# Attention outputs computed transposed, two heads on column halves, with the arena and the opening laid out anew

## The reference

```python
x = layer_norm(ALPHA * x + 0.5 * swiglu_ffn(x, ffn1_w_up, ffn1_w_down), ln1_g, ln1_b)
x = layer_norm(ALPHA * x + hybrid_mixer(x, ...), ln2_g, ln2_b)
x = layer_norm(ALPHA * x + 0.5 * swiglu_ffn(x, ffn2_w_up, ffn2_w_down), ln3_g, ln3_b)
```

```python
logits = where(valid, q . k * scale + bias, -1e30)
p = softmax(logits)
y = sum over keys of p * v
```

## Time and profile before

| | |
|---|---|
| time, median of 3 runs | 1142.32 us (1141.85 to 1142.46) |
| the profiled execution | 1143.03 us; span in the trace 1141.1 us |
| granted TensorE clock, mean | 0.998 |
| TensorE busy | 1128.2 us, 99% |
| VectorE, ScalarE, GpSimd busy | 764.8, 556.1, 409.2 us |
| matmuls of `split_mm` with `xh`, `xl` (lines 712 to 714) | 1236.6 us of busy time, overlapping |
| the same with `hh`, `hl` | 419.0 us |

### The profile page before, as it was taken

One profiled execution on the slowest core, in us unless ns is written; L12 is line 12 of the kernel. 1 busy time (PEld: TensorE's weight loads), 2 busy tenths in 40 slices (PEclk: granted clock), 3 DMA queues, 4 the chain that ended last, 5 costly groups with the idle time before them and its releaser, 6 DMA issues.

```text
span 1141.1 us, 17628 instructions
## 1 busy us (share of the span) xinstructions
PE 1128.2 (99%) x5916; PEld 923.9 (81%) x5916; DVE 764.8 (67%) x1078; ACT 556.1 (49%) x799; POOL 409.2 (36%) x567
## 2 busy tenths in 40 slices
PE   8999999999999999999999999999999999999997
PEld 6788887878788888887788888888777888888885
DVE  5666845789976866685486465468898687655544
ACT  5544542575573455453245454335846635454530
POOL 2789976107710378997700000001276000000001
PEclk9999999999999999999999999999999999999999
DMA  8856653645555575666357566536435466757541
GB/s 266 236 183 195 216 193 111 192 144 160 161 181 196 172 232 177 193 217 201 115 176 227 186 223 199 186 98 222 162 118 183 148 202 199 223 166 242 186 145 37
DMA packets 158719, 207.50 MB, mean 182 GB/s; under 512 B 13144, under 2 KB 107672, under 8 KB 158656
## 3 DMA queue, kind: packets, MB, share of 16 engines
q1 hardware_dynamic: 154928, 201.70, 55.3%
q10 hardware_dynamic: 2704, 3.36, 1.1%
q0 software_dynamic: 1024, 1.61, 0.8%
HBM read 205.56 MB, written 1.06 MB: 181 GB/s over the span
## 4 chain that ended last, share of the span: by engine, by line
PE 87%; DVE 7%; DMA 2%; issue 2%; ACT 1%; SPq 0%; POOLq 0%; POOL 0%; DVEq 0%; ACTq 0%
PE ps L712 27%; PE ps L714 26%; PE ps L713 26%; DVE wlo L1147 3%; PE ps L739 2%; DMA raw<-in_ffn_w_up 1%; DMA raw<-in_w_in 1%; PE ps L977 1%; PE ps L906 1%; PE ps L729 1%; DVE score L1304 1%; PE ps L924 1%; DVE x L1205 1%; PE ps L957 0%; DVE x L1197 0%
## 5 line engine op out<-in xcount | busy, mean ns | idle before, releaser
L1147 DVE TENSOR_TENSOR wlo<-raw,whi 128x1024 fp32r<-128x1024 f32 (+1 forms) x372 | 485.5, 1324 | 191.4 <-ACT whi L405 177.3
L405 ACT CAST whi<-raw 128x1024 fp32r<-128x1024 f32 (+1 forms) x372 | 385.7, 1044 | 300.1 <-PE ps L714 238.5
L712 PE MATMUL ps<-whi,xh 128*128 128x512 f32 (+1 forms) x1056 | 418.5, 396 | 3.3 <-DVE wlo L1147 2.8
L714 PE MATMUL ps<-whi,xl 128*128 128x512 f32 (+1 forms) x1056 | 409.4, 388 | 0.0
L713 PE MATMUL ps<-wlo,xh 128*128 128x512 f32 (+1 forms) x1056 | 408.7, 387 | 0.0
L712 PEld LDWEIGHTS ps<-whi,xh 128*128 128x128 f32 x1056 | 198.4, 188 | 48.4 <-DVE wlo L1147 6.9
L714 PEld LDWEIGHTS ps<-whi,xl 128*128 128x128 f32 x1056 | 198.2, 188 | 41.4
L713 PEld LDWEIGHTS ps<-wlo,xh 128*128 128x128 f32 x1056 | 198.6, 188 | 37.2
L1511 POOL TENSOR_TENSOR rstd<-var_eps,cst 128x1 f32<-128x1 f32 x12 | 18.2, 1518 | 533.6 <-DVE var_eps L1194 533.6
L712 PE MATMUL ps<-whi,hh 128*128 128x512 f32 x352 | 141.3, 401 | 0.0
L714 PE MATMUL ps<-whi,hl 128*128 128x512 f32 x352 | 138.9, 395 | 0.0
(11 more groups left out here) (185 smaller groups left out, 1086.6 us busy)
## 6 DMA issues: line engine op xcount, KB each, us to landing
raw<-in_ffn_w_up SPq DMA_DIRECT2D x352, 256.0 KB, 4.0
raw<-in_ffn_w_down SPq DMA_DIRECT2D x176, 256.0 KB, 3.0
raw<-in_w_in SPq DMA_DIRECT2D x128, 256.0 KB, 3.4
raw<-in_w_branch SPq DMA_DIRECT2D x32, 256.0 KB, 3.2
raw<-in_w_out SPq DMA_DIRECT2D x32, 256.0 KB, 4.2
bias_g<-bias_rows ACTq DMA_DIRECT2D x16, 192.0 KB, 3.9
raw<-in_w_in SPq DMA_DIRECT2D x16, 148.0 KB, 2.3
affine<-in_ln_g SPq DMA_DIRECT2D x4, 512.0 KB, 5.4
```

The source lines that it names most:

```text
L405: nc.scalar.copy(whi[:, s % RING, 0:w], raw[:, s % RAW, 0:w]).then_inc(S["hi_done"], 1)
L712: nc.tensor.matmul(o, ah, bh, start=start, stop=False)
L714: return nc.tensor.matmul(o, al, bh, start=False, stop=stop)
L1147: nc.vector.tensor_tensor(wlo[:, s % RING, 0:w], raw[:, s % RAW, 0:w], f32(whi[:, s % RING, 0:w]), ALU.subtract).then_inc(S["split_done"], 1)
```

## The change

**Attention.** `att_values` swaps the operands: 64 columns of values are the stationary operand, the transposed probabilities move, and the output is head dimension x queries. The even head of a pair goes to partitions 0 to 63 of the output and the odd one to 64 to 127, of the same bank. Key block 0 serves all 256 queries, key block 1 the second 128: four matmuls of 256, 256, 128, 128 columns where there were six of 64. Since a row of the output is no longer a query, the reciprocals are applied before the transposes: `normalize` on ScalarE scales `prob` in place. `ya`, its 8 transposes and `att_out` go. `ya_hi` and `ya_lo` work per pair, straight from the values' bank, in the slots. `prob_transpose` moves from slot 6 to 7 + 4p and `att_values` from 7 to 9 + 4p; the transposes wait for `prob_ready` (normalized) and for pair p - 1's `ya_split`. ScalarE's order in a slot is now copies of the transposed probabilities, exponentials, normalization, high half; VectorE's `invert` and `ya_lo` are placed between splits, those of pairs 1 and 0 inside the third state turn, which starts in slot 7.

**Arena.** Its start is moved up to the weight ring's place modulo 512 bytes.

**Opening.** TensorE's `opening` takes each of chunk 0's tiles for both token halves before the next, with the transposes of x's second half after the first tile's first use; then chunk 1. SyncE loads x's second half after two tiles; ScalarE and VectorE take it after two splits. The bias product and the parameters' transpose are put into `prepare_bank` and come after chunk 0.

```diff
-SCORES_AT, TRANSPOSE_AT, VALUES_AT = 3, 6, 7
+SCORES_AT, TRANSPOSE_AT, VALUES_AT = 3, 7, 9
...
     raw = sb("raw", [P, RAW, QW])
+    ring_at = (nc.sbuf_base + 31) // 32 * 32
...
     arena = (nc.sbuf_base + 31) // 32 * 32
+    arena += (ring_at - arena) % 512
...
-    ya = place("ya", [P, NT, D_ATTN])
...
-                    up_chunk(l, 0, s0 + 4 * c, w_up, c)
                     if n == 0 and c == 0:
+                        up_chunk(l, 0, s0, w_up, 0, range(2))
                         sp.dma_start(x[:, 1, :], A["x"][0, tok(1), :]).then_inc(x_landed[2], 16)
+                        up_chunk(l, 0, s0, w_up, 0, range(2, 4))
+                    else:
+                        up_chunk(l, 0, s0 + 4 * c, w_up, c)
...
-            def att_out(l, p):
-                act.wait_ge(S["pv_done"], N_PAIRS * l + p + 1)
+            def normalize(l, p):
                 act.wait_ge(S["inv_ready"], N_PAIRS * l + p + 1)
                 for hd in (2 * p, 2 * p + 1):
                     for i in range(NT):
-                        a, at = NT * hd + i, (NT * (hd % 2) + i) * HEAD_DIM
-                        ins = nc.scalar.mul(ya[:, i, hd * HEAD_DIM:(hd + 1) * HEAD_DIM],
-                                            ps[:, PV, at:at + HEAD_DIM], inv_sum[:, a:a + 1])
-                ins.then_inc(S["ya_done"], 1)
-
-            def ya_hi(l, t):
-                act.wait_ge(S["yat_done"], NT * l + t + 1)
-                nc.scalar.copy(ya_h[:, :, tok(t)], ps[:, TB - t, :].rearrange("p (k n) -> p k n", k=4)
-                               ).then_inc(S["yah_done"], 1)
+                        a = NT * hd + i
+                        part = prob[:, hd % 2, i * P:i * P + KEYS[i]]
+                        ins = nc.scalar.mul(part, part, inv_sum[:, a:a + 1])
+                ins.then_inc(S["prob_ready"], 1)
+
+            def ya_hi(l, p):
+                act.wait_ge(S["pv_done"], N_PAIRS * l + p + 1)
+                nc.scalar.copy(ya_h[:, p, :], ps[:, PV, 0:SEQ]).then_inc(S["yah_done"], 1)
...
                 for j in range(SLOTS):
-                    if (j - SCORES_AT) % 4 == 0:
-                        p = (j - SCORES_AT) // 4
-                        if 0 <= p < N_PAIRS:
-                            exp_probs(l, p)
-                            if p == N_PAIRS - 1:
-                                load_table(ACT.Gelu_apprx_tanh)
-                    if (j - VALUES_AT) % 4 == 0 and 0 <= (j - VALUES_AT) // 4 < N_PAIRS:
-                        att_out(l, (j - VALUES_AT) // 4)
-                    if (j - TRANSPOSE_AT) % 4 == 0 and 0 <= (j - TRANSPOSE_AT) // 4 < N_PAIRS:
-                        prt_read(l, (j - TRANSPOSE_AT) // 4)
+                    p, rest = divmod(j - TRANSPOSE_AT, 4)
+                    if rest == 0 and 0 <= p < N_PAIRS:
+                        prt_read(l, p)
+                    p, rest = divmod(j - SCORES_AT, 4)
+                    if rest == 0 and 0 <= p < N_PAIRS:
+                        exp_probs(l, p)
+                    if rest == 1 and 0 <= p < N_PAIRS:
+                        normalize(l, p)
+                        if p == N_PAIRS - 1:
+                            load_table(ACT.Gelu_apprx_tanh)
+                    p, rest = divmod(j - VALUES_AT, 4)
+                    if rest == 0 and 0 <= p < N_PAIRS:
+                        ya_hi(l, p)
                     if j in GATE_TILES:
                         splits(s + GATE_TILES[j], 1)
...
             x_hi(0, 0)
-            splits(0, 8)
+            splits(0, 2)
             x_hi(0, 1)
+            splits(2, 6)
...
+            def opening(prep):
+
+                for q, t in ((0, 0), (1, 0), (0, 1), (1, 1), (2, 0), (2, 1), (3, 0), (3, 1)):
+                    if t == 0:
+                        wait_split(q)
+                    if q % 2 == 0:
+                        pe.wait_ge(S["x_ready"], part(0, t, q // 2))
+                    for k in (2 * q, 2 * q + 1):
+                        a, b = (k % 2) * 512, (k % 2) * 512 + 512
+                        ins = split_mm(ps[:, t, :], xh[:, k, tok(t)], xl[:, k, tok(t)], w(whi, q, a, b),
+                                       w(wlo, q, a, b), k == 0, k == KT - 1)
+                    if t == 1:
+                        ins.then_inc(S["pe_used"], 1)
+                    elif q == 3:
+                        ins.then_inc(S["up_done"], 1)
+                    if (q, t) == (0, 0):
+                        x_transpose(0, 1)
+                prepare_bank(0, prep)
+                up_chunk(0, 0, 4, 1, 1, False)
+                h_transpose(0, 0, 0, False)
...
             def prob_transpose(l, p):
-                pe.wait_ge(S["exp_done"], N_PAIRS * l + p + 1)
+                pe.wait_ge(S["prob_ready"], N_PAIRS * l + p + 1)
                 if p > 0:
-                    pe.wait_ge(S["ya_done"], N_PAIRS * l + p)
+                    pe.wait_ge(S["ya_split"], N_PAIRS * l + p)
...
             def att_values(l, p):
                 pe.wait_ge(S["prt_read"], N_PAIRS * l + p + 1)
-                for hd in (2 * p, 2 * p + 1):
-                    for i in range(NT):
-                        at = (NT * (hd % 2) + i) * HEAD_DIM
-                        for k in range(i + 1):
-                            ins = nc.tensor.matmul(ps[:, PV, at:at + HEAD_DIM], prob_t[:, hd % 2, i + k, :],
-                                                   v_sb[:, k, hd * HEAD_DIM:(hd + 1) * HEAD_DIM],
-                                                   start=k == 0, stop=k == i)
+                for k in range(NT):
+                    for e in range(2):
+                        hd, dims = 2 * p + e, slice(HEAD_DIM * e, HEAD_DIM * e + HEAD_DIM)
+                        keys = slice((2 * p + e) * HEAD_DIM, (2 * p + e + 1) * HEAD_DIM)
+                        ins = nc.tensor.matmul(ps[dims, PV, k * P:SEQ], v_sb[:, k, keys],
+                                               prob_t[:, e, 2 * k:2 + k, :], start=k == 0, stop=k == NT - 1)
                 ins.then_inc(S["pv_done"], 1)
...
-                    if m == 0:
-                        ya_transpose(l)
...
-                pe.wait_ge(S["ya_split"], NT * l + 2)
+                pe.wait_ge(S["ya_split"], N_PAIRS * (l + 1))
...
             def ssm_turn(l, q, first=None, second=None):
                 link(nc.vector.tensor_tensor(t, g[:, ::-1], si, ALU.mult))
+                if first is not None:
+                    first()
                 link(nc.vector.tensor_tensor(g, g, co, ALU.mult))
+                if second is not None:
+                    second()
...
-            def ya_lo(l, t):
-                dve.wait_ge(S["yah_done"], NT * l + t + 1)
-                nc.vector.tensor_tensor(ya_l[:, :, tok(t)], ps[:, TB - t, :].rearrange("p (k n) -> p k n", k=4),
-                                        f32(ya_h[:, :, tok(t)]), ALU.subtract).then_inc(S["ya_split"], 1)
+            def ya_lo(l, p):
+                dve.wait_ge(S["yah_done"], N_PAIRS * l + p + 1)
+                nc.vector.tensor_tensor(ya_l[:, p, :], ps[:, PV, 0:SEQ], f32(ya_h[:, p, :]), ALU.subtract
+                                        ).then_inc(S["ya_split"], 1)
...
-                    if rest == 2 and 0 <= p < N_PAIRS:
-                        invert(l, p)
...
                     if j == 3:
-                        splits(s + 21, 3)
-                    if j == 8:
-                        ssm_turn(l, 3)
+                        splits(s + 21, 1)
+                        invert(l, 0)
+                        splits(s + 22, 2)
+                    if j == 7:
+                        ssm_turn(l, 3, lambda: invert(l, 1), lambda: ya_lo(l, 0))
                     if j == 10:
                         ssm_scan(l, 3)
                     if j == 11:
-                        splits(s + 24, 3)
+                        splits(s + 24, 1)
+                        invert(l, 2)
+                        splits(s + 25, 2)
                     if j == 13:
                         splits(s + 27, 1)
+                        ya_lo(l, 1)
                     if j == 14:
                         splits(s + 28, 1)
                     if j == 15:
-                        splits(s + 29, 2)
+                        splits(s + 29, 1)
+                        invert(l, 3)
+                        splits(s + 30, 1)
                     if j == 17:
                         splits(s + 31, 1)
+                        ya_lo(l, 2)
...
+                    if j == 21:
+                        ya_lo(l, 3)
                 splits(s + 35, 1)
-                ya_lo(l, 0)
-                ya_lo(l, 1)
```

More of the change, by code:

```diff
@@ L323, in rows, with up_chunk @@
                 return raw[:, s % RAW, 0:2 * w].rearrange("p (t n) -> p t n", t=2)
-            def up_chunk(l, i, s, w, c):
-                for q in range(4):
+            def up_chunk(l, i, s, w, c, tiles=range(4)):
+                for q in tiles:
                     dst = raw[:, (s + q) % RAW, :].rearrange("p (t g n) -> p t g n", t=2, g=2)
@@ L384, in _ @@
                     wide(mix(l, OUT0 + k), w_out[l], k)
```

(60 more changed lines are left out.)

8 lines of the change are left out of this document (1 added, 7 removed).

## The result

The changed kernel takes 1144.84 us (median of 9 runs, 1143.84 to 1147.07), the kernel before 1142.46 in the same comparison: a ratio of 1.0023, with a 95% interval of 1.0013 to 1.0034. It is slower by 2.4 us, where 0.3 less was forecast. The profiled execution takes 1144.69, with a span of 1142.6.

A forecast was written before the change was run, and what follows sets the result against it. TensorE's issued work was taken to bound the kernel; opening -2.7, arena -5.8 and both mixers +8.2 sum to -0.3, taking the median from 1142.32 to 1142.0 us. Its own range was 1138 to 1146, with rivals 1131 to 1148.

The forecast's parts named there:

- What bounds the kernel: Whole span: TensorE, busy over 99%, sets the end 1 us for 1 us, from the opening to the last normalization.
- The opening: First chunk's weight tiles: using each for both token halves removes TensorE's waiting; gain 2.7 us, bounds 1.3 and 2.8.
- The prediction's last rival: Opening: it does nothing, because the input's second half lands late; +1.4 us, no chance given.
- The arena: Down projections and attention branches: the new start modulo 512 saves 5 ns in 1152 matmuls; gain 5.8 us.
- Rival B: Arena matmuls: the 5 ns come from something else, such as engines beside them; +5.5 us, 1147.8; 12%.
- TensorE's list: Attention slots: value products at 0.85 us and no `ya` transposes take 2.7 us per layer off TensorE, 5.4 in all.
- The waits: Probabilities' transposes, layer 0: TensorE waits 1.7, 3.2 and 1.5 us for normalization and VectorE's low halves; 6.4 in all.
- Rival A: Attention slots of both mixers: the waits don't come; 1128.4 us, or 1135 with half the waits; 25%.
- C: State branch and values: late rotation makes the last `ssm_out` wait, value products don't overlap; +3 us per layer, 1148; 8%.
- +4.5. Both mixers: +8.2: Layer 1's mixer slower by 4.5 us, from layer 0's 3.7 adjusted for tile 25's timing; both layers +8.2 us.

The follow-up runs named there:

- after_padded: The changed kernel with 24 more warm-up matmul pairs in TensorE's program, to move its instruction fetch; 1147.10 us, ratio 1.004.
- attention_only: The kernel before with only the attention changed, the arena and the opening as before; 1152.33 us, ratio 1.0089.
- after_filled: The changed kernel with 76 identity transposes added in TensorE's waits ahead of the probabilities' transposes; 1142.53 us, ratio 1.0.
- arena_opening: The kernel before with the arena and the opening changed and its old attention; 1134.56 us, ratio 0.9929.
- table_late: The changed kernel with ScalarE's splits and VectorE's low halves reordered and ScalarE's table load right ahead of the GELU; 1132.43 us, ratio 0.9913.
- requeued_padded: The changed kernel with ScalarE's splits and VectorE's low halves reordered, plus 24 more warm-up matmul pairs in TensorE's program; 1135.56 us, ratio 0.9944.

## Why the prediction was wrong

**What bounds the kernel: right.** TensorE is busy 98% of the span, and the six waits showed in the time. Not every wait did: where the one at line 918 went (`after_padded`), the end of the slots came no earlier.

**The opening: right.** Forecast 2.7; 2.98 at the first down projection in the table (`attention_only`, with nothing changed up to there, is 0.44 early at that point), 2.3 between medians. The input's second half was issued at 3.69 instead of 4.0, and no tile was late for it. The prediction's last rival, that the opening does nothing, has the wrong size: +1.4 is what its lower bound of 1.3 would cost, nothing at all would have been +2.7.

**The arena: right, by a rule that was too narrow.** Forecast 5.8; 5.6 between medians, 5.0 in the table's three stretches that it touches (-0.84, -2.40 and -1.74). The Trainium skill ("SBUF — State Buffer", section "Who interferes with whom") has no room for it: one port for moving data, another for weights, contention only between VectorE and GpSimd. By that the place would be worth nothing; the runs of four places show that it is worth 5 ns in each of these matmuls, 390 against 395. Rival B is out.

**TensorE's list: right.** 0.80 for a value product against 0.85.

**The waits: right in place, order and nearly in size.** Forecast 1.7, 3.2 and 1.5 in layer 0. By TensorE's starts, against the 2.87 that twelve matmuls take undisturbed, they are 0.9, 3.1 and 2.0: 6.0 against 6.4. The first is shorter because tile 25 landed 0.8 earlier, on before's clock, than the prediction took from the earlier trace rows; from its split on, the first two intervals are as forecast. Layer 0's mixer costs 3.5 for 3.7. Rival A, that the waits don't come, is out; the last `ssm_out` made nobody wait, so C is out as well.

**The step that failed** is layer 1's, "+4.5. Both mixers: +8.2". Layer 1 cost 6.0, 1.5 more. On the clock of its own mixer's start the split of tile 25 comes 0.2 later than I took it; the interval from the second to the third transposes is 0.6 longer than forecast (pair 3's exponentials end 4.8 behind the middle low half in layer 0, not 4.2, and the normalization and all behind it with them; in layer 0 the early tile had hidden this); and 0.7 is the granted clock. A wait was priced as idle time alone, and no term stood for what TensorE's clock does behind it. The runs show that term to be the one without a fixed size: 0.7 in the changed kernel's trace, 1.7 in that of `after_padded`, and runs of that kernel 6 us apart with the mean clock from 0.997 to 0.990.

The 0.2 at tile 25 hides a second thing that was taken from before unasked: when its tile lands. `after_filled`, whose clock stays and whose fetch is elsewhere, costs 3.4 in the same mixer. Of the 2.6 to the changed kernel's 6.0, 0.7 is the clock, and tile 25, 1.8 earlier there on the mixer's own clock, is the rest. `after_padded`, where only the fetch was moved, has it 1.1 earlier. So in `after_filled`, with neither effect, the layer is 1.1 cheaper than the forecast, and that 4.5 came as near 6.0 as it did is in part luck.

Summed in the table: opening -3.0, arena -5.0, mixers +3.5 and +6.0, +1.5 at the end of the span. The forecast's same sum was -2.7 - 5.8 + 3.7 + 4.5 = -0.3. Of the 1.8 between them 1.5 is layer 1's, and of the arena's 0.8 the opening and layer 0 make 0.5 good. Between medians the miss is larger, 1142.0 against 1144.84: the prediction took the profiled run to be 0.7 above the median, as in before, and the changed kernel's is 0.15 below it. The time lies inside the range of 1138 to 1146 and on the other side of no change; a forecast of -0.3 that is the difference of 8.5 and 8.2 had no hold on its sign.

The Trainium skill ("TensorE: Matmul & The Clock Gate", section "Part 1: The HAM clock gate (the "warmup" mystery)") says that an idle TensorE falls to the lower of its clocks. Layer 1 agrees, 0.50 behind an idle stretch of 2.96; layer 0, behind one of the same 2.96, stays at 1.00, and so does layer 1 of `attention_only`. Why the clock falls behind one of two equal waits and not behind the other no run here shows; that filling the waits keeps it is what `after_filled` shows.

**What stays open besides.** Against `arena_opening`, `table_late` wins 2.3 us of the 2.7 that leave TensorE's list in layer 0, and 0.7 in layer 1; what holds back the rest there is open. Value products in a bank of their own, which would take the wait for the low half away, are not shown either.

## What to carry to other kernels

When a change lets a saturated TensorE wait in the middle of a stage, price the wait and what follows it: look at the granted clock window by window behind the longest one, and look at the scatter of the runs, which was 2 us for the kernel before and 3 and 6 us for two with long waits (it was 3 us for `requeued_padded` too, so it is a hint and no proof). Idle matmuls put into an unavoidable wait are a cheap test of it. A stage whose end hangs on one tile's landing gains nothing from an engine that arrives earlier: find the instruction from which the distances stay the same. Where parts with opposite signs travel together, time them apart: two of these gave 8.0 us, and the third gave its own 2.1 (1134.56 to 1132.43) only once every queue that it passes through had been put in order again.

## What the runs showed of the hardware

- A 128x512 matmul of this kind starts every 227 or every 232 ns by where its stationary operand begins: 0 and 256 bytes past the ring's place modulo 512 are fast, 64 and 384 slow.
- The count of TensorE's instructions ahead of a tight stretch matters: 24 fewer moved the fetch of a 16 KB block from 809.3 in the trace of before to 814.3, onto the weight tiles, and a tile took 6.2 us to land instead of 4.2. 24 more moved it away, to 806.6.
- TensorE's clock can fall to 0.50 behind an idle stretch of 2.96 us and can stay at 1.00 behind an equal one; both are in one trace. With 76 transposes of the identity in the waits it stayed at 0.998 or 0.999 in all 11 runs.
- Two products on two column halves, 2 x 256 and 2 x 128 columns in float32, take 0.80 us where six of 64 columns took 1.36.
